# SSD y products: a second PSUM bank for the second head group, and state products issued over four array quadrants

## The reference

```
cb      = einsum(C, B)                                  # per group
y_diag  = einsum(cb * decay_in, x*dt)                   # per head: contraction over 128 tokens
y_off   = einsum(C, h_prev) * exp(a_cum)                # per head: contraction over 64 states
y       = y_diag + y_off + d * x
```

## Time and profile before

| what | us |
| --- | --- |
| median of 3 runs (lowest to highest) | 1873.46 (1869.45 to 1873.93) |
| the profiled execution, its own time | 1874.78 |
| its span, first to last instruction | 1873.0 |
| TensorE busy | 1802.6 |
| VectorE, ScalarE, GpSimd busy | 685.2, 384.3, 494.0 |

### The profile page before, as it was taken

One profiled execution on the slowest core, in us unless ns is written; L12 is line 12 of the kernel. 1 busy time (PEld: TensorE's weight loads), 2 busy tenths in 40 slices (PEclk: granted clock), 3 DMA queues, 4 the chain that ended last, 5 costly groups with the idle time before them and its releaser, 6 DMA issues.

```text
span 1873.0 us, 28638 instructions
## 1 busy us (share of the span) xinstructions
PE 1802.6 (96%) x11549; PEld 1736.5 (93%) x11549; DVE 685.2 (37%) x1402; ACT 384.3 (21%) x925; POOL 494.0 (26%) x483
## 2 busy tenths in 40 slices
PE   6989999999999999799999999999999999999996
PEld 6989999999988898688899999999999999999996
DVE  5837811318133434776763341121111111111125
ACT  5322121332123213433311131100110011001111
POOL 4452122222211111111123332233223322332231
PEclk9999999999999988899999999999999999999998
DMA  5473363232232223433363322233223422342233
GB/s 188 78 136 108 103 193 92 93 94 80 94 114 80 92 80 108 136 105 115 119 212 120 107 67 91 90 115 110 90 90 101 124 90 92 109 134 90 90 115 135
DMA packets 80784, 205.00 MB, mean 109 GB/s; under 512 B 15648, under 2 KB 35360, under 8 KB 80440
## 3 DMA queue, kind: packets, MB, share of 16 engines
q1 hardware_dynamic: 38192, 89.83, 15.9%
q0 software_dynamic: 20912, 72.39, 12.8%
q10 hardware_dynamic: 21592, 41.56, 7.0%
HBM read 179.05 MB, written 24.48 MB: 109 GB/s over the span
## 4 chain that ended last, share of the span: by engine, by line
PE 85%; DVE 5%; issue 3%; ACT 2%; DMA 2%; POOL 1%; ACTq 1%; SPq 0%; DVEq 0%; POOLq 0%
PE ps L1108 26%; PE ps L1109 25%; PE ps L1110 25%; POOL WL L842 1%; PE ps L1444 1%; DMA gate_scratch<-GT 1%; PE ps L1475 1%; PE ps L1480 1%; DMA WRAW<-in_w 1%; DVE X L2121 1%; PE ps L1313 1%; PE ps L1603 1%; PE ps L1527 1%; ACT SB L1964 1%; PE ps L1309 1%
## 5 line engine op out<-in xcount | busy, mean ns | idle before, releaser
L1108 PE MATMUL ps<-HL,WH 128*128 128x384 f32 (+1 forms) x2496 | 826.8, 331 | 17.1 <-ACT GT L1670 7.2
L1109 PE MATMUL ps<-HH,WL 128*128 128x384 f32 (+1 forms) x2496 | 813.5, 326 | 0.0
L1110 PE MATMUL ps<-HH,WH 128*128 128x384 f32 (+1 forms) x2496 | 811.8, 325 | 0.0
L1108 PEld LDWEIGHTS ps<-HL,WH 128*128 128x128 f32 x2496 | 475.1, 190 | 29.2 <-issue 22.3
L1109 PEld LDWEIGHTS ps<-HH,WL 128*128 128x128 f32 x2496 | 475.4, 190 | 0.2
L1110 PEld LDWEIGHTS ps<-HH,WH 128*128 128x128 f32 x2496 | 474.8, 190 | 0.0
L842 POOL TENSOR_TENSOR WL<-WRAW,WH 128x1024 fp32r<-128x1024 f32 x133 | 328.2, 2468 | 487.1 <-DMA WH<-in_w 487.1
L839 POOL DMA_DIRECT2D WH<-in_w x133 | 77.0, 579 | 759.6 <-PE ps L1110 749.0
L2113 DVE TENSOR_TENSOR FM<-FS,ps 128x384 f32<-128x384 f32 (+1 forms) x66 | 34.3, 521 | 436.7 <-PE ps L1110 432.7
L1108 PE MATMUL ps<-FL,WH 128*128 128x384 f32 (+1 forms) x528 | 171.7, 325 | 6.8 <-POOL WL L842 6.7
L1110 PE MATMUL ps<-FH,WH 128*128 128x384 f32 (+1 forms) x528 | 170.9, 324 | 0.0
(11 more groups left out here) (319 smaller groups left out, 1626.2 us busy)
## 6 DMA issues: line engine op xcount, KB each, us to landing
WRAW<-in_w SPq DMA_DIRECT2D x145, 512.0 KB, 3.3
WH<-in_w POOLq DMA_DIRECT2D x136, 512.0 KB, 3.7
gate_scratch<-GT ACTq DMA_DIRECT2D x24, 528.0 KB, 3.1
PX<-gate_scratch ACTq DMA_DIRECT2D x24, 528.0 KB, 3.6
X<-in_x ACTq DMA_DIRECT2D x8, 528.0 KB, 5.4
X<-in_x SPq DMA_DIRECT2D x16, 192.0 KB, 4.8
u_scratch<-UF ACTq DMA_DIRECT2D x4, 528.0 KB, 4.6
GF<-gelu_scratch SPq DMA_DIRECT2D x4, 528.0 KB, 5.1
```

Of the source, the lines that this page charges most:

```text
L1108: nc.tensor.matmul(out, wh, rl, start=start, stop=False)
L1109: nc.tensor.matmul(out, wl, rh, start=False, stop=False)
L1110: return nc.tensor.matmul(out, wh, rh, start=False, stop=stop)
```

## The change

The four heads of group 1 write bank 6 instead of bank 7, in the same columns and partitions as the heads of group 0 in bank 7. The eight heads are done in two halves: four y_diag products (two heads of each group), then four y_off products in an order in which each goes to another quadrant of the array. The fence is gone. Because bank 6 is also the target of the next chunk's E products of group 1, these wait for `ye_ok`. VectorE reads the second half of y from bank 6.

```diff
             for g in range(2):
                 if n >= 1:
                     pe.wait_ge(l_ok, n)
+                    if g == 1:
+                        pe.wait_ge(ye_ok, n)
                 for k in range(4):
...
-            for i in range(4):
-                g = i // 2
-                if i == 2:
-                    fence_set(last)
-                heads = [(2 * i + j, (2 * i + j) % 4, bank[7][64 * j:64 * j + 64, i * P:i * P + rows]) for j in range(2)]
-                for h, k, o in heads:
+            def y_at(h):
+                i, j = divmod(h, 2)
+                return bank[7 - i // 2][64 * j:64 * j + 64, (i % 2) * P:(i % 2) * P + rows]
+
+            for p in range(2):
+                heads = [4 * g + 2 * p + j for j in range(2) for g in range(2)]
+                for h in sorted(heads):
                     m = L[0:rows, h, 0:rows] if not smp else LS[:, 1, h, :]
-                    nc.tensor.matmul(o, XS[0:rows, h * HD:(h + 1) * HD], m, start=True, stop=smp)
-                if i == 2:
-                    fence_wait()
+                    nc.tensor.matmul(y_at(h), XS[0:rows, h * HD:(h + 1) * HD], m, start=True, stop=smp)
                 if not smp:
-                    for h, k, o in heads:
-                        last = nc.tensor.matmul(o, HS[64 * g:64 * g + 64, n % 2, k, :], CD[64 * g:64 * g + 64, k, :],
-                                                start=False, stop=True)
+                    for h in heads:
+                        r, k = 64 * (h // 4), h % 4
+                        last = nc.tensor.matmul(y_at(h), HS[r:r + 64, n % 2, k, :], CD[r:r + 64, k, :], start=False, stop=True)
                 else:
                     for b in range(NSEQ):
-                        for h, k, o in heads:
+                        for h in heads:
...
-                yi = bank[7][:, i * P:i * P + rows]
+                yi = bank[7 - i // 2][:, (i % 2) * P:(i % 2) * P + rows]
```

More of the change, by code:

```diff
@@ L1467, in ssd_chunk @@
                 pe.wait_ge(ye_ok, n)
-            for i in range(4):
-                g = i // 2
-                if i == 2:
-                    fence_set(last)
-                heads = [(2 * i + j, (2 * i + j) % 4, bank[7][64 * j:64 * j + 64, i * P:i * P + rows]) for j in range(2)]
-                for h, k, o in heads:
+            def y_at(h):
[4 more added lines that the diff above has]
+                for h in sorted(heads):
                     m = L[0:rows, h, 0:rows] if not smp else LS[:, 1, h, :]
-                    nc.tensor.matmul(o, XS[0:rows, h * HD:(h + 1) * HD], m, start=True, stop=smp)
-                if i == 2:
-                    fence_wait()
+                    nc.tensor.matmul(y_at(h), XS[0:rows, h * HD:(h + 1) * HD], m, start=True, stop=smp)
                 if not smp:
-                    for h, k, o in heads:
-                        last = nc.tensor.matmul(o, HS[64 * g:64 * g + 64, n % 2, k, :], CD[64 * g:64 * g + 64, k, :],
-                                                start=False, stop=True)
+                    for h in heads:
+                        r, k = 64 * (h // 4), h % 4
+                        last = nc.tensor.matmul(y_at(h), HS[r:r + 64, n % 2, k, :], CD[r:r + 64, k, :], start=False, stop=True)
                 else:
                     for b in range(NSEQ):
-                        for h, k, o in heads:
-                            last = nc.tensor.matmul(o[:, b:SMP:NSEQ], H0[64 * g:64 * g + 64, b, k, :],
-                                                    CD[64 * g:64 * g + 64, 0, k * SMP + b:(k + 1) * SMP:NSEQ],
+                        for h in heads:
+                            r, k = 64 * (h // 4), h % 4
+                            last = nc.tensor.matmul(y_at(h)[:, b:SMP:NSEQ], H0[r:r + 64, b, k, :],
+                                                    CD[r:r + 64, 0, k * SMP + b:(k + 1) * SMP:NSEQ],
                                                     start=False, stop=True, skip_group_check=True)
```

## The result

The changed kernel took 1859.01 us in the median of 6 runs (1852.94 to 1861.26), the kernel before 1871.86 beside it (6 runs, 1869.45 to 1873.93). The ratio is 0.9926, with a 95% interval of 0.9906 to 0.9945: 13.8 us less, give or take 3.6. Forecast were 10.8 less and 1862.7, which was reckoned from a median of 1873.46. Two more rounds of the unaltered changed kernel gave 0.9921 (0.9898 to 0.9943) and 0.9913 (0.9900 to 0.9926), with medians of 1857.27 and 1855.19. Over all runs of this study the mean is 1871.7 before (69 runs, standard deviation 3.0) and 1857.0 after (16 runs, 2.7), so 14.7 less.

The account below looks back on a forecast made before the run. TensorE's queue was taken to bound the kernel. Eight prompt chunks gave 8.2 us and the sample chunk 2.6, with fence, wait and clock at 0: 10.8 less, from 1873.46 to 1862.7 us, range 1858 to 1869.

Parts of the forecast that it names:

- TensorE's queue sets the end of the stage: SSD stage: TensorE is busy 96% of the span, so a microsecond taken from its queue there counts in full.
- Anatomy of a group: y products: a pair of records costs 0.11 us, a change of tile form adds 0.05 at entry and 0.10 at exit.
- Four quadrants at once: y_off groups: eight records in four quadrants take 0.37 us; prompt chunk 1.87 instead of 2.89, sample chunk 2.76 instead of 5.34.
- Rival 2: y_off products: only two quadrants run at a time, gain 5.3 us, total 1868.2; chance 0.09.
- rival 3: y_off: four at a time in prompt chunks but not with the sample chunk's 4 columns; gain 8.9, total 1864.6; chance 0.08.
- The floor of about 25 ns between starts: Sample chunk: if it held over all tiles together, a y_off group's 64 records would take at least 1.6 us.
- The fence was hidden: Fence before the sixth of a chunk's eight y groups: costs nothing today, so removing it is worth 0.
- the added wait is hidden: Next chunk's fifth E product: starts 1.2 us after VectorE has read y, so the wait costs 0.
- Nothing is given back later: Stages behind the SSD stage: the forecast let the stage's whole gain of 10.8 us reach the total.
- Rival 4: Stages behind 710 us wait for something the stage doesn't move; total within 0.3% of before, say 1870; chance 0.06.
- The clock at 0 in the forecast: Gate third behind the sample chunk: up to 2.9 us from a full clock was possible, but counted as 0.
- rival 1: Behind the sample chunk: no clock fall after the shorter thin stretch, another 2.9 us, total 1859.8; chance 0.20.

Follow-up runs that it names:

- e4: Changed kernel with all eight y_diag products, then all eight y_off products, instead of two halves; 1856.93 us, 0.9919 of the kernel before.
- e6: Kernel before with the second bank, no fence and the added wait, in the old order of products; 1868.38 us, 0.9978 of the kernel before.
- e8: Changed kernel with the wait for VectorE's read of y moved ahead of the next chunk's first product; 1876.65 us, 1.0022 of the kernel before.
- e12: Kernel before, without any edit, timed and profiled again; 1870.66 us, ratio 1.0000.
- e5: Changed kernel's grouping alone: all heads in bank 7, a fence between the two groups' y_off products, no added wait; 1868.95 us, 0.9994 of the kernel before.
- e1: Changed kernel, unaltered, timed and profiled a second time; 1857.27 us, 0.9921 of the kernel before.
- e11: Changed kernel, unaltered, timed and profiled a third time; 1855.19 us, 0.9913 of the kernel before.
- e7: Changed kernel with y_off products in sorted head order, both of group 0, then both of group 1; 1856.88 us, 0.9929 of the kernel before.

## Why the prediction was right, point by point

- *TensorE's queue sets the end of the stage.* Shown. The four forms of this queue at full clock (172.8, 162.5, 159.8, 155.2) differ by what the counted groups differ. The totals go down by 14.7 and by another 6.8 where the stage goes down by 10.3 and 7.3; the 2.7 of e4 can't be seen in the total.
- *Anatomy of a group: 0.11 a pair of records, 0.15 a change of form.* Read from the 2.89 of before, and shown by 1.88, 1.58 and 0.98 in three other orders. The prediction calls the change of form half of the 0.37; by its own numbers it is 0.15 of it, two fifths, and the sum uses 0.15. The Trainium skill has "Mode switching requires drain" ("TensorEngine Tiling (Array Packing)", Key Properties). It gives no price; the rows do, though they do not show that a drain is what costs the 0.15.
- *Four quadrants at once.* Shown in both forms of product, by 0.45 for eight records and 1.11 for 64. Rival 2 and rival 3 are out. In the sample chunk 64 records have their starts within 0.9 us (1.11 less the 0.20 of the last), 0.015 each. The floor of about 25 ns between starts, cited in the prediction from the Trainium skill ("TensorE: Matmul & The Clock Gate"), does not hold over tiles taken together. The trace of before already had that, more plainly than the prediction read it: the first two y_diag records of a chunk, at 573.96, are 0.28 long together and 0.27 each, so they start 0.01 apart.
- *The fence was hidden, the added wait is hidden.* Shown by e6, and by e8, which puts a price on the wait once it isn't.
- *Nothing is given back later.* Rival 4 is out by the totals, which went down by more than the stage did. Three profiles of the same kernel scatter by 5 behind the stage, so a smaller amount could be given back unseen.
- *The clock at 0 in the forecast.* This is the mis-sized term. Of the 10.8 that were forecast, 10.5 are work at full clock (8.2 and 2.3) and 0.3 the lower clock in the last y_off group; 10.3 came at full clock. Over all runs the kernel is 14.7 faster, so 4.4 are not in the counted work. The prediction's step said that a thin stretch had been followed by the lower clock before, and left it at that.

Behind the sample chunk it is half told. In the four profiles with the old times (before, e12, e5, e6) the fall there starts 0.7 to 2.3 us ahead of the gate third, is 6.8 long, and the gate third takes 6.4 to 7.2 us. In those with the new (changed, e1, e11, e7) 3.4, 3.4, 3.4 and 0 us of the gate third are at 1.2 GHz, and it takes 5.96, 5.96, 5.96 and 4.42. But where the gate third was spared, the next fall, right behind the stage, was longer: 10.2 us in e7, against 6.8 in the changed kernel.

```profile
687.60:694.40 6.80, 6.64 (x25) 5.31 (x24) 4.21 (x9) 3.03 (x3) 0.00 (x0) 0.50 0.44 173
```

```profile
685.80:695.90 10.10, 8.88 (x34) 5.95 (x31) 6.52 (x14) 3.04 (x3) 0.00 (x0) 0.50 0.46 169
```

So rival 1 came half, worth about 3.4 × 0.45 = 1.5 us, and not more in e7. The rest is argued. The mean granted clock over whole runs is 0.9808 in 63 runs of before and 0.9832 in 16 of the changed kernel. By span that is 71.9 and 62.4 us at 1.2 GHz, 9.5 less with a standard error of 1.7, of which the stage accounts for about 5 (10.2 in each of the four old profiles; 3.4, 10.2, 3.4 and 3.4 in the new). At 0.45 each the 9.5 would be 4.3 us. That price is for a TensorE without gaps; among the 75 runs of before and its copy, a run with 1 us more at 1.2 GHz is only 0.33 longer (standard error 0.04), which makes it 3.1. Either figure leaves no more than the scatter between kernels seen in e5 and e6. Why the changed kernel has less of that time in stages that it doesn't touch is open, and no experiment here moved the clock alone. That the first round's median still fell inside the range is in part luck: the range allowed about a microsecond for the clock beyond rival 1, and the two later rounds lie outside.

## What to carry to other kernels

Group small products by tile form, and give row tiles that should run together banks of their own: on this kernel neither did anything by itself, and both together took a third off the y products. Count such a place in steps (here 0.11 us a pair of passes) and changes of form (0.15 us), from the distances between starts; the sum held to a hundredth without fences and to 0.05 with them. Price a wait by what stands between the producer and the first instruction that needs it. Idle time beside thin products cost twice here, once by itself and once by the clock.

## What the runs showed of the hardware that was not expected

- An idle gap of 1.3 us in each chunk raised the time at 1.2 GHz in the stage from 3.4 to 23.9 us; in the profiled execution it cost 11.3 us by itself and 9 more by the clock (20.5 × 0.45). Over ten runs the total rose by 18.7 and the time at 1.2 GHz, over the whole span, by 17 (79.8 against 62.4).
- With 4 columns the pace is not a fixed time for each product: 64 records in four quadrants take 1.11 us, 32 in two quadrants 1.10, and at 1.2 GHz 32 take 1.87.
- Four products of two passes each, in four quadrants, take the two steps of one, in either order of the heads: 0.45 us in the changed kernel and in e7. In both traces their first four records start within 0.02 us, and the other four from 0.16 on.
